# Nine blocks a layer of the down projection as seven block products

## The reference, cut

```python
for l in range(DEPTH):                      # DEPTH = 2
    y = mixer_sublayer(x, w_in[l], ...)
    x = layer_norm(ALPHA * x + y, ln1_g[l], ln1_b[l])
    # conv_ffn: h = silu(conv(x @ w_gate)) * (x @ w_up), 256 x 5632
    y = h @ w_down[l]                       # 5632 x 2048
    x = layer_norm(ALPHA * x + y, ln2_g[l], ln2_b[l])
```

## Time and profile before

| | |
|---|---|
| device time, median of 3 runs | 2224.84 us (2224.28 to 2224.9) |
| the profiled execution: span | 2222.5 us; its device time is not recorded apart from the runs', whose median lies 2.3 above the span |
| TensorE busy | 2208.0 us, 99%, 11424 matmuls |
| VectorE, ScalarE, GpSimd busy | 1397.8, 1037.8, 244.1 us |
| HBM | 189 GB/s over the span |
| first down stage | 868.3 to 1107.8 us |
| second down stage | ends with TensorE's last matmul, 2213.5 us |

### The profile page before, as it was taken

The page is one execution under the profiler, slowest core; times in us unless marked ns, Lnnn a source line. Parts: engine busy times, 40 slices in busy tenths (PEclk is TensorE's granted clock), DMA queues, the critical chain, the costliest instruction groups (busy, mean ns, idle before and its releaser), DMA issues.

```text
span 2222.5 us, 28282 instructions
## 1 busy us (share of the span) xinstructions
PE 2208.0 (99%) x11424; PEld 1892.6 (85%) x11424; DVE 1397.8 (63%) x1758; ACT 1037.8 (47%) x1295; POOL 244.1 (11%) x250
## 2 busy tenths in 40 slices
PE   9999999999999999999999999999999999999998
PEld 7888888888888888888888888888888888888886
DVE  6655576776667666544485566677766666664545
ACT  5444555444444444433454445554444444443343
POOL 1751000220000000000008410002200000000000
PEclk9999999999999999999999999999999999999999
DMA  8655565666666666666665555756666666666664
GB/s 278 194 167 160 157 215 174 189 190 190 190 190 189 190 189 205 219 192 193 190 190 170 162 162 150 225 173 189 189 190 189 190 189 190 189 211 215 191 195 155
DMA packets 214818, 420.92 MB, mean 189 GB/s; under 512 B 13056, under 2 KB 15136, under 8 KB 213664
## 3 DMA queue, kind: packets, MB, share of 16 engines
q1 hardware_dynamic: 211824, 406.37, 59.8%
q0 software_dynamic: 2432, 12.22, 1.6%
q10 hardware_dynamic: 432, 0.52, 0.1%
HBM read 416.97 MB, written 2.10 MB: 189 GB/s over the span
## 4 chain that ended last, share of the span: by engine, by line
PE 98%; DVE 1%; DMA 0%; ACT 0%; issue 0%; POOLq 0%; POOL 0%; SPq 0%; DVEq 0%
PE ps L1289 29%; PE ps L1177 16%; PE ps L1175 16%; PE ps L1176 16%; PE ps L1293 15%; PE ps L1220 1%; PE ps L1416 1%; PE ps L1390 1%; PE ps L1367 1%; DMA raw<-in_w_in_dram 0%; PE ps L1423 0%; PE ps L1163 0%; PE ps L1436 0%; PE ps L1437 0%; PE ps L1435 0%; PE ps L1454 0%
## 5 line engine op out<-in xcount | busy, mean ns | idle before, releaser
L820 DVE TENSOR_TENSOR wlo<-raw,whi 128x1024 fp32r<-128x1024 f32 x767 | 964.7, 1264 | 700.6 <-ACT whi L578 697.0
L578 ACT ACTIVATE whi<-raw 128x1024 fp32r<-128x1024 f32 x767 | 807.9, 1059 | 853.0 <-DMA raw<-in_w_down_dram 278.5
L1289 PE MATMUL ps<-xT,whi 128*128 128x512 f32 x2816 | 657.3, 390 | 0.0
L1289 PEld LDWEIGHTS ps<-xT,whi 128*128 128x128 f32 x2816 | 522.6, 188 | 104.3 <-ACT qkT L599 0.4
L1175 PE MATMUL ps<-whi,xT 128*128 128x512 f32 x920 | 369.0, 401 | 0.0
L1177 PE MATMUL ps<-whi,xT 128*128 128x512 f32 x920 | 359.3, 391 | 0.0
L1176 PE MATMUL ps<-wlo,xT 128*128 128x512 f32 x920 | 358.5, 390 | 0.0
L1293 PEld LDWEIGHTS ps<-xT,wlo 128*128 128x128 f32 x2816 | 350.6, 192 | 7.5
L1293 PE MATMUL ps<-xT,wlo 128*128 128x256 f32 x2816 | 352.9, 283 | 0.0
L1175 PE MATMUL ps<-whi,hT 128*128 128x512 f32 x696 | 270.9, 389 | 0.0
L1177 PE MATMUL ps<-whi,hT 128*128 128x512 f32 x696 | 270.9, 389 | 0.0
(11 more groups left out here) (203 smaller groups left out, 1203.5 us busy)
## 6 DMA issues: line engine op xcount, KB each, us to landing
raw<-in_w_gate_dram SPq DMA_DIRECT2D x176, 512.0 KB, 4.0
raw<-in_w_up_dram SPq DMA_DIRECT2D x176, 512.0 KB, 4.0
raw<-in_w_down_dram SPq DMA_DIRECT2D x176, 512.0 KB, 4.1
raw<-in_w_in_dram SPq DMA_DIRECT2D x175, 512.0 KB, 3.7
raw<-in_w_out_dram SPq DMA_DIRECT2D x64, 512.0 KB, 4.2
xres<-in_x_dram POOLq DMA_DIRECT2D x4, 512.0 KB, 5.7
lnb<-in_ln_g_dram POOLq DMA_DIRECT2D x2, 1024.0 KB, 7.5
lnb<-in_ln_b_dram POOLq DMA_DIRECT2D x2, 1024.0 KB, 10.4
```

Source lines behind the costliest of these rows:

```text
L578: act.activation(whi[:, s, :, :], raw[:, s, :, :], ACT.Copy).then_inc(hi_done, 1)
L820: dve.tensor_tensor(wlo[:, s, :, :], raw[:, s, :, :], whi[:, s, :, :].bitcast(F32), ALU.subtract)\
L1289: return pe.matmul(ps[:, bank, :], whi[:, s, kk, m * P:(m + 1) * P], xT[:, kt, :, :].rearrange("p a s -> p (a s)"), start=kt == 0, stop=kt ...
```

## The change

Nine times a layer a *pair* (one pair of k tiles, 256 rows of w_down) and a half of the columns (two chunks, 1024) leaves the groups and becomes a *set*. Its h part is a 2 x 2 matrix of 128 x 128 tiles (A11, A12 ... first index the token tile, second the k tile), its weight part a 2 x 2 matrix of 128 x 512 tiles (B11 ...: k tile, chunk), and the product is made with seven block products (Winograd's form of Strassen) in place of eight, each three matmuls of 512 columns. Five pairs in the first half, four in the second; 88 groups become 70 and nine sets. `SETS_AT` says after which groups of the stage the sets stand, `SET_LOAD` after which group each is fetched: right behind the set before it.

- SyncE loads the four B tiles of a set (2 x 512 KB) into sraw (in xT's place), which has room for one set.
- GpSimd makes the four sums T1 to T4 (`set_sum`), ScalarE the seven high parts in shi (`set_high`, steps a+6 to a+8 for a set fetched after group a), VectorE the seven low parts, over sraw (`set_low`, steps a+7 to a+9).
- VectorE makes the sums S1 to S4 of the h tiles once for each of five pairs (`form_sums`, `form_low`), ScalarE their high parts (`form_high`).
- TensorE does the set (`set_of_products`), into banks 0 and 1, 2, and 4 to 7. VectorE adds these banks to xres at the end of each half (`products`, beside `y_chunk`): 4 and 7 operations.
- GpSimd loads both rows into lnb2 after the last set.

The diff, cut:

```diff
-GROUPS = BASE_DOWN + NC_OUT * GD
+SETS_AT = ((11, 16, 20, 24, 28), (36, 41, 46, 51))
+SETS = [(half, i) for half in range(2) for i in range(len(SETS_AT[half]))]
+SET_AFTER = [SETS_AT[half][i] for half, i in SETS]
+SET_LOAD = [-1] + SET_AFTER[:-1]
+HALF_GROUPS = [2 * (GD - len(a)) for a in SETS_AT]
+DOWN = sum(HALF_GROUPS)
+DOWN_ENDS = [HALF_GROUPS[0] // 2, HALF_GROUPS[0], HALF_GROUPS[0] + HALF_GROUPS[1] // 2, DOWN]
+PREPARED = len(SETS_AT[0])
+PRODUCTS = ("A12", "S4", "A11", "S1", "S3", "S2", "A22")
+FACTORS = ("B21", "B22", "B11", "T1", "T3", "T2", "T4")
+SLOT = {"B11": 0, "B12": 1, "T3": 1, "B21": 2, "B22": 3, "T1": 4, "T2": 5, "T4": 6}
+TARGET = (0, 2, 4, 5, 7, 6, 1)
+SUMS = (((4,), (4, 6, 5)), ((4, 6, 7), (4, 6, 7, 5)))
+GROUPS = BASE_DOWN + DOWN
+def down_group(n):
+    c = next(c for c in range(NC_OUT) if n < DOWN_ENDS[c])
+    first = (0, *DOWN_ENDS)[c]
+    return c, n - first, n - first + len(SETS_AT[c // 2])
...
+        sraw = nc.alloc_sbuf_tensor_at("sraw", [P, 7, CW], F32, offset=xT_at)
+        slo = nc.alloc_sbuf_tensor_at("slo", [P, 7, CW], F32R, offset=xT_at)
+        shi = nc.alloc_sbuf_tensor_at("shi", [P, 7, CW], F32R, offset=xT_at + 7 * CW * 4)
+        hsum = nc.alloc_sbuf_tensor_at("hsum", [P, GK, SEQ], F32, offset=xT_at + 14 * CW * 4)
+        hform = nc.alloc_sbuf_tensor_at("hform", [P, 4, P], F32, offset=xT_at + 15 * CW * 4)
+        forms = nc.alloc_sbuf_tensor_at("forms", [P, 3 * PREPARED + 1, 2, P], F32R, offset=mix_at)
...
+        def third_form(pair):
+            if pair < len(SETS_AT[1]):
+                return hT[:, GK * pair, :, P:SEQ]
+            return forms[:, 3 * PREPARED + pair - len(SETS_AT[1]), :, :]
+        def operand(pair, name):
+            if name == "S3":
+                return third_form(pair)
+            if name in ("S1", "S2", "S4"):
+                return forms[:, 3 * pair + ("S1", "S2", "S4").index(name), :, :]
+            t, kk = int(name[1]) - 1, int(name[2]) - 1
+            return hT[:, GK * pair + kk, :, t * P:(t + 1) * P]
...
-                for two in range(0, NC_OUT // 2):
-                    for half in range(2):
-                        col = two * (2 * CW) + half * CW
-                        for j in range(GD):
-                            load(w_down, layer, two * (2 * GD), BASE_DOWN + half * GD + j, j * GK, col)
+                for n in range(DOWN):
+                    c, _, pair = down_group(n)
+                    load(w_down, layer, 0, BASE_DOWN + n, pair * GK, c * CW)
+                    if n - RING in SET_LOAD:
+                        k = SET_LOAD.index(n - RING)
+                        half, pair = SETS[k]
+                        if k == 0:
+                            wait_groups(sp, layer, BASE_DOWN)
+                        if layer + k > 0:
+                            sp.wait_ge(set_used, set_count(layer, k - 1))
+                        for kk in (1, 0):
+                            row = (GK * pair + kk) * P
+                            sp.dma_start(sraw[:, 2 * kk:2 * kk + 2, :].rearrange("p s n -> p (s n)"),
+                                         w_down[layer, row:row + P, half * 2 * CW:(half + 1) * 2 * CW])\
+                                .then_inc(set_in, 16)
...
+            def set_sum(layer, k):
+                done = 4 * (set_count(layer, k) - 1)
+                pool.wait_ge(set_in, 32 * set_count(layer, k))
+                slot = lambda name: sraw[:, SLOT[name], :]
+                pool.tensor_tensor(slot("T1"), slot("B12"), slot("B11"), ALU.subtract).then_inc(set_sums, 1)
+                pool.wait_ge(set_sums, done + 1)
+                pool.tensor_tensor(slot("T3"), slot("B22"), slot("B12"), ALU.subtract).then_inc(set_sums, 1)
+                pool.tensor_tensor(slot("T2"), slot("B22"), slot("T1"), ALU.subtract).then_inc(set_sums, 1)
+                pool.wait_ge(set_sums, done + 3)
+                pool.tensor_tensor(slot("T4"), slot("B21"), slot("T2"), ALU.subtract).then_inc(set_sums, 1)
...
+                for k in range(len(SETS)):
+                    set_sum(layer, k)
                 pool.wait_ge(h_done, layer * PAIRS + PAIRS)
+                pool.wait_ge(set_used, set_count(layer, len(SETS) - 1))
                 carry_wait(pool, 3)
                 pool.dma_start(lnb2[:, 0, :], row(ln2_g, layer).broadcast_to([P, D_MODEL])).then_inc(ln2_in, 16)
-                wait_groups(pool, layer, BASE_DOWN + GD // 2)
                 pool.dma_start(lnb2[:, 1, :], row(ln2_b, layer).broadcast_to([P, D_MODEL])).then_inc(ln2_in, 16)
...
+            def set_high(layer, k, part):
+                names = (FACTORS[0:2], FACTORS[2:5], FACTORS[5:7])[part]
+                for name in names:
+                    if name[0] == "T":
+                        act.wait_ge(set_sums, 4 * (set_count(layer, k) - 1) + ("T1", "T3", "T2", "T4").index(name) + 1)
+                    elif name == "B21":
+                        act.wait_ge(set_in, 32 * set_count(layer, k))
+                    act.activation(shi[:, SLOT[name], :], sraw[:, SLOT[name], :], ACT.Copy).then_inc(set_hi, 1)
+            def form_high(layer, pair):
+                act.wait_ge(hform_done, 3 * pair_count(layer, pair))
+                act.activation(forms[:, 3 * pair:3 * pair + 3, 0, :], hform[:, 0:3, :], ACT.Copy)
+                act.activation(third_form(pair)[:, 0, :], hform[:, 3, :], ACT.Copy).then_inc(hform_hi, 1)
+            def set_steps(layer, n):
+                for k, a in enumerate(SET_LOAD):
+                    if k < PREPARED and n == max(a + 6, 8):
+                        form_high(layer, k)
+                    part = n - max(a + 6, 8)
+                    if 0 <= part < 3:
+                        set_high(layer, k, part)
...
                 cols = slice(c * CW, (c + 1) * CW)
+                if which == 1 and c % 2 == 0:
+                    dve.wait_ge(set_used, set_count(layer, (PREPARED, len(SETS))[c // 2] - 1))
                 for t in range(TT):
+                    if which == 1 and c % 2 == 1:
+                        dve.tensor_tensor(xres[:, t, cols], xres[:, t, cols], ps[:, banks[t], :], ALU.add)\
+                            .then_inc(psum_free[banks[t]], 1)
+                        continue
                     dve.scalar_tensor_tensor(xres[:, t, cols], xres[:, t, cols], ALPHA, ps[:, banks[t], :],
                                              ALU.mult, ALU.add).then_inc(psum_free[banks[t]], 1)
+                if which == 1 and c % 2 == 0:
+                    return
                 for t in range(TT):
...
+            def products(layer, c):
+                cols = slice(c * CW, (c + 1) * CW)
+                if c % 2 == 0:
+                    for t in range(TT):
+                        wait_read(dve, layer, in_banks(c)[t], ("down", c))
+                for i in range(4):
+                    for t in range(TT):
+                        banks = SUMS[t][c % 2]
+                        if i >= len(banks):
+                            continue
+                        if i == 0 and c % 2 == 1:
+                            ins = dve.scalar_tensor_tensor(xres[:, t, cols], xres[:, t, cols], ALPHA,
+                                                           ps[:, banks[i], :], ALU.mult, ALU.add)
+                        else:
+                            ins = dve.tensor_tensor(xres[:, t, cols], xres[:, t, cols], ps[:, banks[i], :], ALU.add)
+                        link(ins)
+                if c % 2 == 1:
+                    for b in (4, 5, 6, 7):
+                        dve.nop().then_inc(psum_free[b], 1)
+                else:
+                    for t in range(TT):
+                        last = dve.bn_stats(stats[:, t, c, :], xres[:, t, cols])
+                    link(last)
+            def form_sums(layer, pair):
+                count = pair_count(layer, pair)
+                k0 = GK * pair
+                if count > 1:
+                    dve.wait_ge(hform_lo, count - 1)
+                dve.tensor_tensor(hsum[:, :, :], hT[:, k0:k0 + GK, 0, :].bitcast(F32),
+                                  hT[:, k0:k0 + GK, 1, :].bitcast(F32), ALU.add).then_inc(hsum_done, 1)
+                dve.wait_ge(hsum_done, count)
+                a11, a21, a12, a22 = hsum[:, 0, 0:P], hsum[:, 0, P:SEQ], hsum[:, 1, 0:P], hsum[:, 1, P:SEQ]
+                dve.tensor_tensor(hform[:, 0, :], a21, a22, ALU.add).then_inc(hform_done, 1)
+                dve.tensor_tensor(hform[:, 3, :], a11, a21, ALU.subtract)
+                dve.wait_ge(hform_done, 3 * count - 2)
+                dve.tensor_tensor(hform[:, 1, :], hform[:, 0, :], a11, ALU.subtract).then_inc(hform_done, 1)
+                dve.wait_ge(hform_done, 3 * count - 1)
+                dve.tensor_tensor(hform[:, 2, :], a12, hform[:, 1, :], ALU.subtract).then_inc(hform_done, 1)
+            def form_low(layer, pair):
+                dve.wait_ge(hform_hi, pair_count(layer, pair))
+                dve.tensor_tensor(forms[:, 3 * pair:3 * pair + 3, 1, :], hform[:, 0:3, :],
```

(104 more changed lines are left out.)

5 lines of the change are left out of this document (2 added, 3 removed).

## The result

The changed kernel takes 2254.66 us in the median (four runs, 2254.05 to 2258.53) against 2224.82: a ratio of 1.0138, 95% interval 1.0124 to 1.0151. It is slower by 29.8 us. Forecast were 2248.4, in a range of 2224 to 2274.

A forecast was written before the change was run, and what follows sets the result against it. TensorE, busy in 99% of the span, was taken as the bound. Removing 54 matmuls saves 12.2 us and stalls on late sets add 35.8, so 2224.84 + 23.6 = 2248.4 us, in a range of 2224 to 2274.

The forecast's parts named there:

- sets 2, 3, 4 (gap 4): First half of the down stage, four groups between sets: each set ends 4.2 us late, 12.6 a layer.
- set 5 (gap 8): Joint of the halves: VectorE's additions and splits delay y_chunk(1), which frees bank 2 1.7 us late, once a layer.
- The landing: SyncE's two 512 KB loads into the single buffer: second lands at T + 5.1, bounds T + 4.3 and T + 5.8.
- T: Time when TensorE could start the group behind the previous set; the buffer is free at T + 0.2.
- The sums: GpSimd's four serial weight sums: 5.3 us, plus 1.14 for a VectorE split that excludes them on the shared port.
- form_low: VectorE's low parts of the h sums, first half only: some 0.8 us added ahead of the subtractions.
- D: When VectorE can start a set's subtractions: T + 12.5 first half, T + 11.7 second; set ends D + 7.4.
- The order of seven subtractions and two splits: VectorE work behind D: seven subtractions at 0.61 and two splits at 1.14 between them, 6.55 us.
- The clock: TensorE's granted clock in the down stages: expected to stay 1.00, with a longest idle piece of 2.3 us.
- signs of being wrong: Profile after: sums under 5 us, sets landing under 4, PE waits naming a bank or ScalarE, down-stage clock under 1.00.
- rival 4: TensorE's clock falls in the stalls; six gap-4 sets cost 29 us more if pitch doubles: 2277 us, chance 0.04.
- Rival 1: Each set's factors are ready in time, so all 12.2 us is won: 2212.6 us, chance 0.05.

The follow-up runs named there:

- e8: The change with SETS_AT (9, 14, 19, 24, 29), (37, 42, 47, 52), subtractions together except set 5's, y_chunk(1) two steps later: 2214.79 us, 0.9957 of the kernel before.
- e6: The change with GpSimd's four sums on 8 of 512 columns behind one memset, so products are not the down projection: 2222.24 us, 0.999 of the kernel before.
- e9: The change with form_low one step earlier (a+6), ahead of the factors' landing: 2252.6 us, 1.0132 of the kernel before.
- e2: The change with a set's seven subtractions together in step a+7, not over three steps with splits between: 2250.33 us, 1.0116 of the kernel before.
- e3: The change with every gap of 4 made 5 (first sets at 8, 13, 18, 23, 28) and the seven subtractions together: 2218.72 us, 0.9975 of the kernel before.
- e5: The change with ten matmuls of zeros ahead of the wait for form_low in sets 2 to 4: 2253.28 us, 1.0128 of the kernel before.

## Why the prediction came out as it did

The direction, the range and the mechanism were right: a single buffer whose factors take some 19.7 us from free to used. The size was 6.3 us low in the medians. Step by step, with stalls read as the distance of two set ends less the matmuls between, both layers of the profiled execution, which is 3.9 us above the median:

| term | forecast | measured |
|---|---|---|
| 54 matmuls at 0.2267 | -12.2 | -12.2 (group pitch 2.72 as before; e8) |
| sets 2, 3, 4 (gap 4), six | 25.2 | 29.2 |
| set 1 (gap 5), two | 3.0 | 2.8 |
| sets 6 to 8 (gap 5), six | 4.2 | 7.8 |
| set 5 (gap 8), two | 3.4 | 5.9 |
| sum | +23.6 | +33.6 (spans: +34.2; medians: +29.8) |

Of the 29.2, some 4 are the two sets at a long low clock; without them the gap-4 sets come to the 25.2 of the forecast, and what is left of the miss is sets 6 to 8 and set 5 (3.6 and 2.5). That the median runs lack these 4 us is likely from their mean clock (0.996 against 0.992), but no trace of one was taken.

- *The landing* was the term mis-sized most widely: L = T + 5.1 by the pitch in a backlog. Read at the start of the first sum it is T + 5.5 to 6.3 in fifteen of sixteen sets, with a median of T + 5.8, the upper bound of the forecast, and T + 6.75 in one. From issue to landing the median is 4.9 us, where 3.7 is that of a single load in the trace of before. In the second half, which has no forms, that is most of the 0.6 a set between 0.7 and 1.3.
- *The sums*: 5.3 + 1.14 = 6.4 forecast, 6.4 measured at set 2 (931.87 to 938.31) and 6.15 to 6.5 over all, the exclusion included; e6 shows their weight.
- *form_low* was counted at 0.8 behind the sums and cost 0.3 (e9). With the late landing D is T + 12.0 to 12.6 in the first half, T + 12.5 forecast: two errors that cancelled, and so it is luck that the gap-4 sets come out as forecast. The end of the set is D + 7.5, T + 20.0 at set 2.
- *The order of seven subtractions and two splits* held: without the splits between, a set at full clock needs 17.7 in place of 19.7 (e2), and at a gap of 5 no set but 0 and 5 is late (e3).
- *The clock* is where a statement was wrong. The idle piece ahead of A12 was forecast at 2.3 us and is 1.8 to 2.4 in the six; the forecast was 1.00 all the same, because the only fall in the trace of before stood behind a longer idle time. The clock falls in all six gap-4 sets, one of the forecast's own signs of being wrong. Its price, though, is not that of rival 4 (29 us): two sets of the profiled execution end 2 us later than their like (21.85 and 21.97 apart), with the factors landed and their low parts done about as early as in the others, and e5, which keeps the clock, is 1.4 us faster in the median. That execution, at 2258.5, is also the slowest of the four, at a mean clock of 0.992 against 0.996. The slow matmuls also fill the shorter waits behind the splits, so the profile lists 20.3 us of waits on slo where 30 to 36 were forecast.
- *Set 5* waits on bank 2 and on split 36, as named, 1.3 us longer on average. The layers differ: 2.2 us in the first, with the landing at T + 5.6 and no fall of the clock, 3.7 in the second, with the landing at T + 6.75 and a fall. The landing, 1.2 later, is most of that difference; how much is the clock wasn't taken apart. (A wait on a bank stood among the signs of being wrong, though the forecast's own sum for set 5 has one.)
- *Rival 1* is dead in this kernel (no set came in time), but not as a plan: e3 and e8 make it true with another order, without a further buffer.

## What to carry to other kernels

When a scheme with fewer matmuls needs prepared operands, write down the time from "buffer free" to "operand ready" as a chain (landing, each serial operation, each operation that the preparing engine owes others in between) and compare it with the matmuls between two uses; the share of busy time (VectorE 67%, GpSimd 16%) says nothing of it. Here that chain was some 19.7 us, the matmuls 15.6 to 18.4, and the saving of 0.7 a set was lost up to seven times over (29.2 over six sets is 4.9 each). Shorten the chain's order first (subtractions together: 2 us) and give each use the distance that is left; then look at the joints between stages, where the same engine has a heap of other work.

## What the runs showed of the hardware

TensorE's clock went to its lower level behind idle pieces of 1.8 to 2.4 us, in a stage in which it is else busy all the time, seven times out of seven in the kernel after; ten matmuls of zeros ahead of the wait for form_low kept it at 1.00 in all gap-4 sets (e5). The length of the piece alone doesn't decide: in e9 the clock fell behind 2.20 us and stayed up behind 3.06. A product at the lower level had its matmuls 0.43 us apart in place of 0.23. What that costs depends on the slack around it: next to nothing where each product waits for its factor, 1.7 to 1.9 us a set in e2, where it doesn't.

An operation of VectorE with two SBUF inputs that meets one of GpSimd waits for it inside its own duration: a subtraction of 128 columns shows 1.35 us in place of 0.28 (the change and e9), a sum on GpSimd 2.28 in place of 1.30. The trace shows no idle time there; only the comparison with the same operation elsewhere does.
